# Output projection of a hybrid transformer block: last four weight panels in buffers of their own, first panel loaded earlier, one fold of the modulation moved behind the mixing

## The reference

```python
ada = (silu(c) @ w_ada + b_ada).reshape(1, 3, 3, 1024)       # chunks 0..8 of 1024
x = layer_norm(ALPHA*x + 0.5*mod(0,2)*swiglu(h, ffn1_w_in, ffn1_w_out), ln1_g, ln1_b)
h = x*(1.0 + mod(1,1)) + mod(1,0)
# token mixer: pooling branch y_a, attention branch y_b, two gates
mixed = sigmoid(g_a)*y_a + sigmoid(g_b)*y_b                  # (512, 1024)
y = mixed @ w_mix_out                                        # the output projection
x = layer_norm(ALPHA*x + mod(1,2)*y, ln2_g, ln2_b)
h = x*(1.0 + mod(2,1)) + mod(2,0)
x = layer_norm(ALPHA*x + 0.5*mod(2,2)*swiglu(h, ffn2_w_in, ffn2_w_out), ln3_g, ln3_b)
```

## Time and profile before

| | before |
|---|---|
| median of 3 runs | 1111.31 us (1110.97 to 1112.39) |
| profiled execution | 1111.36 us |
| its span | 1109.0 us |
| PE busy | 1097.9 us, 99% of the span |
| DVE, ACT, POOL busy | 526.8, 413.6, 536.4 us |
| granted TensorE clock | 0.999 |
| DMA | 142.11 MB, mean 128 GB/s |

### The profile page before, as it was taken

The page is one execution under the profiler, slowest core; times in us unless marked ns, Lnnn a source line. Parts: engine busy times, 40 slices in busy tenths (PEclk is TensorE's granted clock), DMA queues, the critical chain, the costliest instruction groups (busy, mean ns, idle before and its releaser), DMA issues.

```text
span 1109.0 us, 15426 instructions
## 1 busy us (share of the span) xinstructions
PE 1097.9 (99%) x5596; PEld 898.5 (81%) x5596; DVE 526.8 (48%) x914; ACT 413.6 (37%) x666; POOL 536.4 (48%) x283
## 2 busy tenths in 40 slices
PE   9999999999999999999999999999999999999997
PEld 6788888888888997875578887898888888888887
DVE  5677756441121269368747778784322223111105
ACT  5463322323222284378723232357332222232223
POOL 2335544444444364559824453646444444445452
PEclk9999999999999999999999999999999999999999
DMA  9545555332333263200136654323433332233322
GB/s 372 199 156 206 187 181 169 123 105 71 102 105 96 83 237 117 86 25 34 49 122 204 215 178 145 114 77 133 134 132 114 113 113 95 90 91 103 105 69 76
DMA packets 53459, 142.11 MB, mean 128 GB/s; under 512 B 5792, under 2 KB 13984, under 8 KB 52128
## 3 DMA queue, kind: packets, MB, share of 16 engines
q1 hardware_dynamic: 52400, 136.25, 37.1%
q10 hardware_dynamic: 1008, 5.17, 1.3%
HBM read 139.31 MB, written 2.10 MB: 128 GB/s over the span
## 4 chain that ended last, share of the span: by engine, by line
PE 83%; issue 9%; POOL 4%; DVE 2%; ACT 1%; DMA 0%; POOLq 0%; ACTq 0%; DVEq 0%
PE psum L663 25%; PE psum L665 25%; PE psum L664 25%; POOL w_lo L566 4%; PE psum L1044 2%; PE psum L1095 1%; PE psum L1123 1%; PE psum L979 1%; PE psum L693 1%; POOL Pr L610 0%; DMA colv<-in_cols 0%; PE psum L1015 0%; DVE X L2055 0%; DVE X L2038 0%; PE psum L714 0%
## 5 line engine op out<-in xcount | busy, mean ns | idle before, releaser
L566 POOL TENSOR_TENSOR w_lo<-raw,w_hi 128x1024 fp32r<-128x1024 f32 x183 | 451.8, 2472 | 519.9 <-ACT w_hi L1219 519.5
L663 PE MATMUL psum<-h_hi,w_hi 128*128 128x512 f32 (+1 forms) x1008 | 382.1, 379 | 1.3 <-POOL h_lo L615 1.0
L664 PE MATMUL psum<-h_lo,w_hi 128*128 128x512 f32 (+1 forms) x1008 | 378.8, 376 | 0.0
L665 PE MATMUL psum<-h_hi,w_lo 128*128 128x512 f32 (+1 forms) x1008 | 378.6, 376 | 0.0
L1219 ACT ACTIVATE w_hi<-raw 128x1024 fp32r<-128x1024 f32 x183 | 191.9, 1052 | 149.2 <-PE psum L665 95.8
L663 PEld LDWEIGHTS psum<-h_hi,w_hi 128*128 128x128 f32 x1008 | 189.6, 188 | 41.6 <-issue 4.5
L665 PEld LDWEIGHTS psum<-h_hi,w_lo 128*128 128x128 f32 x1008 | 189.7, 188 | 34.7
L664 PEld LDWEIGHTS psum<-h_lo,w_hi 128*128 128x128 f32 x1008 | 189.7, 188 | 33.8
L1907 DVE SCALAR_TENSOR_TENSOR acc<-ada_raw,cact,acc 128x512 f32<-128x512 f32 x98 | 139.4, 1459 | 14.9 <-DMA ada_raw<-in_ada_w 14.9
L663 PE MATMUL psum<-act_hi,w_hi 128*128 128x512 f32 (+1 forms) x396 | 145.3, 367 | 0.0
L665 PE MATMUL psum<-act_hi,w_lo 128*128 128x512 f32 (+1 forms) x396 | 144.7, 365 | 0.0
(11 more groups left out here) (272 smaller groups left out, 1011.2 us busy)
## 6 DMA issues: line engine op xcount, KB each, us to landing
raw<-in_ffn_in SPq DMA_DIRECT2D x82, 512.0 KB, 3.3
ada_raw<-in_ada_w SPq DMA_DIRECT2D x112, 256.0 KB, 3.5
raw<-in_ffn_out SPq DMA_DIRECT2D x32, 448.0 KB, 3.3
raw<-in_mix_w SPq DMA_DIRECT2D x27, 512.0 KB, 3.3
ada_first<-in_ada SPq DMA_DIRECT2D x8, 1024.0 KB, 10.5
raw<-in_ffn_out SPq DMA_DIRECT2D x16, 512.0 KB, 3.5
raw<-in_branch_w SPq DMA_DIRECT2D x8, 512.0 KB, 3.8
raw<-in_mixout_w SPq DMA_DIRECT2D x8, 512.0 KB, 3.4
```

The lines of the kernel that those rows point to most:

```text
L566: gp.tensor_tensor(w_lo[:, slot, :], raw[:, slot % 2, :], w_hi[:, slot, :].bitcast(F32), ALU.subtract).then_inc(split_done, 1)
L663: pe.matmul(o_, w_hi[:, wslot, ws], xh, start=first, stop=False)
L664: pe.matmul(o_, w_hi[:, wslot, ws], xl, start=False, stop=False)
L665: return pe.matmul(o_, w_lo[:, wslot, ws], xh, start=False, stop=last)
```

## The change

There are five edits.

- M4 to M7 (`OWN = 4` panels from `OWN_FROM`) are split into `late_hi` and `late_lo`, which lie where the operands of the branches were. ACT waits for the end of the branches before the first of them (`panels_used` at `B_MIXOUT`). PE takes them from there. F0 to F3 then need from the ring only that M0 to M3 have been used.
- ACT's list: `MIXOUT_SPLIT` says how far the splits go ahead of each `square`. Before it was M3, M4, M5, M6, M7 for m = 0 to 4, and F0 behind; now it is M3, M5, M7, F0, F2. F3 comes behind the first `square_half`, where before F1 to F3 stood later among the parts of the norm.
- POOL's list: all splits up to F3 come ahead of the low parts of h. Before, F3 stood behind the first four of these.
- SP loads M0 ahead of the last six loads of `w_ada`, and not behind them.
- The third fold on DVE stands behind the mixing of the last tile, and `sum_modulation` on PE stands three products into M1, where before it stood ahead of M0.

```diff
+OWN = 4
+OWN_FROM = B_MIXOUT + KT - OWN
+MIXOUT_SPLIT = [4, 6, 8, 9, 11]
...
+        late_hi = at("late_hi", [P, OWN, 1024], R + 57344, F32R)
+        late_lo = at("late_lo", [P, OWN, 1024], R + 73728, F32R)
...
                     branch_panel(i + 2)
+                if i == 3 * KT - 3:
+                    panel(B_MIXOUT, mixout_w[0, :, :], slot=B_MIXOUT % 2)
                 for q in range(2 * (i % 3), 2 * (i % 3) + 2):
                     ada_unit("mix", i // 3, q)
-            for m in range(KT):
+            for m in range(1, KT):
...
+            def own_split(i):
+
+                p = OWN_FROM + i
+                gp.wait_ge(split_hi, p + 1)
+                gp.tensor_tensor(late_lo[:, i, :], raw[:, p % 2, :], late_hi[:, i, :].bitcast(F32),
                                  ALU.subtract).then_inc(split_done, 1)
...
-                    splits(B_BRANCH + 4, end + 3)
+                    splits(B_BRANCH + 4, OWN_FROM)
+                    for i in range(OWN):
+                        own_split(i)
+                    splits(B_FFN2, B_FFN2 + GROUP)
                 for m in (1, 2, 3, 4):
                     low(L, 0, m)
-                split(end + 3, 3)
+                if L == 1:
+                    split(end + 3, 3)
...
             pe.wait_ge(br_mixed, KT - 1)
-            sum_modulation(2, 3, 6)
             for m in range(LATE[2][0]):
+                slot, w = mixout_panel(m)
...
-                    ins = product(bank(m % 2), p % 4, k, mixed_hi[:, k, :], mixed_lo[:, k, :],
-                                  k == 0, k == KT - 1)
+                    ins = product(bank(m % 2), slot, k, mixed_hi[:, k, :], mixed_lo[:, k, :],
+                                  k == 0, k == KT - 1, w)
+                    if m == 1 and k == 2:
+                        sum_modulation(2, 3, 6)
...
-                need(act, panels_used, p - 3)
+                if isinstance(p, int) and OWN_FROM <= p < B_FFN2:
+                    act.wait_ge(panels_used, B_MIXOUT)
+                    act.activation(late_hi[:, p - OWN_FROM, :], raw[:, slot % 2, :], ACT.Copy).then_inc(split_hi, 1)
+                    return
+                if isinstance(p, int) and B_FFN2 <= p < B_FFN2 + OWN:
+                    act.wait_ge(panels_used, p - 3 - OWN)
+                else:
+                    need(act, panels_used, p - 3)
...
                     square_half(L, i, 0)
+                    if L == 2 and i == 0:
+                        split_before(p0 + 1)
...
             for m in range(LATE[2][0]):
-                split_before(B_MIXOUT + m + 1)
+                split_before(B_MIXOUT + MIXOUT_SPLIT[m] - 3)
                 square(2, m)
-            split_before(B_FFN2 - 2)
...
-                    if m == KT - 1 and q % 2:
+                    if m == KT - 1 and q in (1, 3):
...
                 mixed_lo_part(m)
+            dve.wait_ge(ada_used, ADA_BASE["mix"] + 8 * N_ADA["mix"])
+            fold_modulation(2)
             residual(2, 5, 0.5, lambda m: B_MIXOUT + m + 1)
```

More of the change, by code:

```diff
@@ L566, in split @@
                 gp.tensor_tensor(w_lo[:, slot, :], raw[:, slot % 2, :], w_hi[:, slot, :].bitcast(F32),
+                                 ALU.subtract).then_inc(split_done, 1)
+            def own_split(i):
+                p = OWN_FROM + i
+                gp.wait_ge(split_hi, p + 1)
+                gp.tensor_tensor(late_lo[:, i, :], raw[:, p % 2, :], late_hi[:, i, :].bitcast(F32),
                                  ALU.subtract).then_inc(split_done, 1)
@@ L659, in _, with product @@
         def _(pe):
-            def product(o_, wslot, kk, xh, xl, first, last):
+            def product(o_, wslot, kk, xh, xl, first, last, w=(w_hi, w_lo)):
                 ws = slice(kk * P, (kk + 1) * P)
-                pe.matmul(o_, w_hi[:, wslot, ws], xh, start=first, stop=False)
-                pe.matmul(o_, w_hi[:, wslot, ws], xl, start=False, stop=False)
-                return pe.matmul(o_, w_lo[:, wslot, ws], xh, start=False, stop=last)
+                pe.matmul(o_, w[0][:, wslot, ws], xh, start=first, stop=False)
+                pe.matmul(o_, w[0][:, wslot, ws], xl, start=False, stop=False)
+                return pe.matmul(o_, w[1][:, wslot, ws], xh, start=False, stop=last)
             def panel_over_h(p, wslot, b, h_wait=None):
@@ L1166, in _, with mixout_panel @@
                 ins.then_inc(panels_used, 1)
+            def mixout_panel(m):
+                p = B_MIXOUT + m
+                return (p - OWN_FROM, (late_hi, late_lo)) if p >= OWN_FROM else (p % 4, (w_hi, w_lo))
             pe.wait_ge(br_mixed, KT - 1)
-            sum_modulation(2, 3, 6)
             for m in range(LATE[2][0]):
+                slot, w = mixout_panel(m)
                 p = B_MIXOUT + m
@@ L1190, in _ @@
                     for k in range(KT):
-                        ins = product(psum[:, (m + h) % 2, part(h)], p % 4, k, mixed_hi[:, k, part(h)],
-                                      mixed_lo[:, k, part(h)], k == 0, k == KT - 1)
+                        ins = product(psum[:, (m + h) % 2, part(h)], slot, k, mixed_hi[:, k, part(h)],
+                                      mixed_lo[:, k, part(h)], k == 0, k == KT - 1, w)
                         if k == KT - 1:
```

## The result

| | before | after |
|---|---|---|
| median | 1111.32 us (1110.97 to 1112.55) | 1114.41 us (1113.96 to 1115.99, 10 runs) |
| profiled execution | 1111.36 us | 1114.59 us |
| its span | 1109.0 us | 1112.8 us |
| granted TensorE clock | 0.999 | 0.996 |

The ratio is 1.003, with a 95% interval of 1.0022 to 1.0038: the change made the kernel slower by 3.1 us. Forecast were 1113.9 us. One launch of all those behind this document, of the kernel in *Early splits of M4 to M7, late F0*, ran in a slow state, at a mean granted clock of 0.851, took 1216.12 us and is left out.

The account below looks back on a forecast made before the run. PE, busy 99% of the span, was taken as the bound. The terms -1.72 + 3.7 + 1.4 + 0.3 - 1.1 gave +2.6 us on 1111.36, so 1113.9 us; range for 8 in 10: 1109.5 to 1116.0.

Parts of the forecast that it names:

- start, at M2: M0 follows the branches without waiting, 1.94 us won; the small sum inside M1 costs 0.22, leaving 1.72 us gain at M2.
- stall at M6: PE waits for z(4), the residual of tile 4, before M6's first half: 3.7 us, bounds 0 and 4.0.
- late sum, at M7: M7's first half waits for M5's late tile and late sum on DVE: 1.4 us, bounds 0 and 2.
- lower clock in M6: Rival: PE's clock falls to its lower level for one half tile, 2.9 us more, 1116.8 us; 4%.
- F3 on the variance: F3's split on POOL lies on the squares of M6's half and so on the variance: about 0.3 us, 0 to 1.
- low parts of h: Two waits at the second feed-forward vanish as F0 to F3 are already split: 1.1 us back, bounds 0.4 and 1.1.
- rival 5: Nothing acts, since M0 still waits for the last mixing: 1111.3 us; no chance of its own given.
- z(0): Residual of tile 0 ends at 696.6, M2 wants it at 696.70: just in time, lateness counts in full, bounds 0 and 0.5.
- The collision: F0's and F1's splits on POOL each hold one of DVE's three SBUF operations between z(3) and z(4), z(4) at 719.5.
- Rivals 1 and 3: 1: F0 and F1 miss DVE's three operations, 1108.6 us, 13%. 3: F0 also holds a column operation before z(3), 1116, 8%.
- Rival 2: F1 lands over 1 us later and holds nothing, stalls of 1.2 + 1.4 us: 1111.4 us; 17%.

Follow-up runs that it names:

- Early splits of M4 to M7, late F0: Changed kernel, M4 to M7 still split early, F0 behind tile 4's square, F1, F2 behind M6's, M7's half squares, F3 behind the second half's first: 1108.42 us.
- the moved fold alone: Kernel before, with only the fold, `sum_modulation` and M0's load moved: 1109.51 us, ratio 0.9986.
- POOL waits for z(4): Changed kernel, but POOL waits for z(4) before it splits F0; ACT's and SP's lists the same: 1117.68 us, one run.
- PE kept busy: Changed kernel with fourteen needless matmuls in PE's list ahead of M6's first half: 1113.75 us, ratio 1.0025.
- F3 behind the root: Changed kernel, ACT's M4 to F0 one split between two squares, F1, F2 behind M6's, M7's half squares, F3 behind root and second half's first square: 1108.93 us.
- the last experiment: Kernel before, with four needless memsets on POOL ahead of M7's split, begun when z(3) is done: 1110.96 us, ratio 1.0002.
- two subtractions: Kernel before, with two needless SBUF to SBUF subtractions on POOL ahead of M7's split, begun when z(3) is done: 1117.29 us, ratio 1.0052.
- the fold undone: Changed kernel with the moved fold, small sum and M0's load put back to their places: 1115.7 us, ratio 1.004.

## Why the prediction was right, and where not

It gave 1113.9 us (1109.5 to 1116.0); the median is 1114.41. The mechanism, POOL's splits of F0 and F1 on DVE's additions ahead of z(4), was right, and so was the size of its stall; the clock behind it was not foreseen. Starts are given behind the last branch product.

| term | forecast | after | which run shows it alone |
|---|---|---|---|
| start, at M2 | -1.72 | -1.52 (11.53 for 13.05) | the moved fold alone: -1.67 |
| stall at M6 | +3.7 | +3.77 | gone where POOL waits for z(4) |
| late sum, at M7 | +1.4 | covered by the next | PE kept busy: +1.7 (4.59 for 2.87, 1.45 of it the wait) |
| lower clock in M6 | 0 (4% for one half tile) | +2.42 in place of the late sum's | PE kept busy: 0.7 beyond the late sum |
| F3 on the variance | +0.3 | +0.1 (M7 to second feed-forward) | not tried alone |
| low parts of h | -1.1 | -0.8 | F3 behind the root: end of the first four tiles at 70.69 for 71.51 with the moved fold alone |

**The start.** M0 follows the branches without a wait, so rival 5 is out. The sum in M1 cost 0.27 us (11.38 - 5.67 - 5.44 with the moved fold alone), for 0.22. z(0) was called just in time with bounds of 0 and 0.5, and it was late by 0.15: M2 stands 0.38 behind its predecessor. M2 itself then takes 5.58 for 5.44, so at M5 the gain is 1.38. The read-out of the modulation was held as forecast, as DVE's timeline after shows:

```profile
694.00 1.80 DVE L2013 TENSOR_SCALAR mod<-ada 128x8 f32<-128x8 f32 x1
```

**The collision.** This was the step that decided, and it came as worked out. With the 0.26 us added, z(3) ended at 712.92 (712.6 forecast), F0's split began at 713.34 (712.7) and z(4) ended at 719.94 (719.5). The forecast had left open which two of the three operations would be held. It was the second by F0 and the third by F1: the first sum was under way when F0 came. Rivals 1 and 3 hung on F0's moment, which was 0.6 later than given. Rival 2 hung on F1's: ACT was done with it at 715.56 (715.1 forecast), 0.5 later, and it needed over 1 us. One reading was off: the 0.54 us for six column operations covers only five, and here the six take 0.70 (711.22 to 711.92), which z(3) had to spare.

The Trainium skill (SBUF — State Buffer, "Who interferes with whom") states this collision for a DVE operation with two SBUF inputs beside a POOL operation that reads SBUF, and not for one that only writes it. The traces agree, with 2.71 and 2.82 us beside POOL's subtractions here, and with 0.69 beside the memsets of the last experiment. The eight-element operation with one input was held again, 1.80 us at 694.00 beside M3's split, as in the earlier trace rows; no run shows in which mode it ran.

**The clock.** This is the step that failed. The forecast's case held a stall of 3.7 us and left the clock at 1.00 behind it; the fall was a rival with 4%, priced at 2.9 on top of everything. It came in the likeliest case itself, and at a quarter of the price (0.7), since a stretched M6 covered what PE would have waited for the late sum anyway. The Trainium skill (TensorE: Matmul & The Clock Gate, "Loop structure matters more than you think") has such a fall in a long wait. This trace agrees: the mean is 0.86 from 715 to 719.7, where PE's idle time of 3.61 us lies, and 0.50 behind it. I had taken the lack of a row as evidence against it, though the trace of before has no stall of this length that could have shown one.

**The sum.** The steps together are further off than the time is. At the end of the first four tiles of the second feed-forward the changed kernel stands 4.05 us later behind the branches (77.19 for 73.14), where the sum had 2.6: 0.7 from the clock, 0.34 from the start, 0.3 from the late sum, 0.3 from h, less 0.2 for F3. Of the 1.4 us between, 0.26 came back because this execution's branches ended earlier, and 0.6 because less time lies around its span (1.8 us, 2.4 before). Neither is the change's doing: in the ten other profiles the last branch product lies at 684.91 to 686.45, with the moved fold and without. So that the profiled time comes within 0.7 us of the forecast is in part luck. The medians differ by 3.1.

**The low parts of h.** Of two distances of 0.67 and 0.68 one is left:

```profile
740.31 0.28 PE L684 MATMUL psum<-h_hi,w_lo 128*128 128x256 f32 x1
740.74 0.39 PE L682 MATMUL psum<-h_hi,w_hi 128*128 128x256 f32 x1 [0.15 <-POOL h_lo L630]
```

I had them both vanish. With F1 and F2 out of the way, POOL's own `h_lo` is still 0.3 us behind PE's wish once.

## What to carry to other kernels

A split moved ahead on POOL is not free because POOL is idle there: each of these subtractions of 2.4 us held one DVE addition of SBUF tiles to its end, unless the addition had begun first. Lay DVE's list beside it, and keep the stretch between two of DVE's results that PE waits for free of it; here F0's split put off by 3.7 us, with those behind it put off too, turned +3.1 us into -2.5 (*Early splits of M4 to M7, late F0*). And when a stall of several us is forecast for PE, put the lower clock behind it into the sum, but subtract the waits that it covers.

## What the runs showed of the hardware

- The granted clock went to its lower level (0.50) at each of the four idle times of PE of 3.6 to 7.6 us in this stretch: within the idle time and for 6.8 us in three (the changed kernel, POOL waits for z(4), two subtractions), and 0.9 us behind its end and for 3.4 us in one (the fold undone). It stayed at 1.00 at idle times of up to 1.45 us, and where needless matmuls filled the wait.
- DVE additions of 128x512 took 2.4 to 2.9 us where a POOL subtraction of 128x1024 was ahead of them, and 0.69 beside POOL memsets of 0.9 us each. A residual, which reads PSUM and one SBUF tile, kept 0.75 beside either (714.94 in the kernel before, beside M7's split; 714.58 in the kernel with the memsets).
- When DVE waits for a POOL operation to end and POOL has another one ready, DVE goes first: two splits in a row took 5.39 us with a DVE operation between, and three POOL operations held three of DVE's, one each.
